# Forming expert 0's token list by itself, ahead of the gates, in a one-core encoder layer with a grouped top-2 mixture of experts

## The chip, the cores and the metric

The kernel runs on one NeuronCore of a Trainium2 chip. Five engines matter here: TensorE (PE in the profile, with its weight loads as PEld), VectorE (DVE), ScalarE (ACT), GpSimd (POOL) and SyncE (SP), which issues most DMAs. The metric is the device time of one execution in microseconds, lower is better; the number given for a kernel is the median of its runs.

## The reference, cut to what matters

A layer takes 512 tokens (two sequences of 256) of width 1024. The first part is a token mixer; its result, normalised, is `x1`. The second part, which the change touches, sends every token to 2 of 16 experts:

```python
s = sigmoid(x1 @ w_router)                       # 512 x 16
sb = (s + b_router).reshape(-1, 4, 4)            # 4 groups of 4 experts
group = argmax of the sum of the two best sb in each group
idx = the two best experts of that group
w = s[idx] / sum(s[idx])                         # the two gates of the token
for e in range(16):
    h = silu(x1 @ w_e1[e]) * (x1 @ w_e3[e])
    y += gates[:, e] * (h @ w_e2[e])             # gates are 0 where e wasn't chosen
```

The kernel doesn't compute all tokens with all experts. For each expert it forms a list of at most 128 tokens that chose it, gathers their rows, computes those, and scatters the results. (A second part for experts with more than 128 tokens stands behind a branch that this input doesn't take.)

## The kernel before

**What comes ahead.** The token mixer takes the first 440 us. TensorE then turns and multiplies the normalised rows with the router weights, and the scores of all tokens reach VectorE at 452.3 us. SyncE writes `x1` to DRAM (`x1_scratch`), since the rows of an expert are gathered from there.

**Selection, on VectorE (lines 1435 to 1478).** Small operations on 128 partitions by 16 to 64 elements make `r_sel` (1 where a token chose an expert, line 1447). From it come the gates (`w_sum`, `w_inv`, `gates`), the rank of the expert among the chosen (`r_kth`), and the table `info`, with four columns for each token and expert: the token's number plus one, which of its two choices it is, and the gate in two parts. TensorE makes `position` from `r_sel` meanwhile: the place of each token in each expert's list (lines 2103 and 2106). A token chooses from one group only, so `joint` adds the four groups' positions for the k-th expert of a group: one `onehot` matrix (token by place) then serves experts k, 4+k, 8+k and 12+k together.

**Lists.** A product of a `onehot` with `info` (`joint_slots`, line 2117: four matmuls for one k, one for each tile of 128 tokens) gives for each place of the list the token, the choice and the gate, for four experts. `fill_lists` on VectorE turns this into `list_token` (the gather's indices), `list_row` (where results go) and `list_gate`. Places without a token get a number out of bounds. In the kernel before, both first one-hots are made, then the lists of k=0 and of k=1 follow, each with its own product; those of k=2 and k=3 come later, while TensorE computes expert 0.

**Gather.** GpSimd clears `xg` (a memset of both buffers, line 1767) once `x1` is stored, and then gathers the rows of expert 0 and expert 1 (`gather`, line 1751), each as soon as its list is there (`token_ready`). TensorE turns the gathered rows (`turn_xg`, line 2137), ScalarE rounds them to `xgT_hi`, VectorE makes the rest `xgT_lo` (`split_xg`, line 1541). Every product of the expert stage needs both parts, of the rows and of the weights.

**Experts.** From there TensorE computes the experts one after the other: 12 units of weights each (512 KB a unit), which SyncE loads, ScalarE rounds to `w_hi` (line 719) and VectorE completes with `w_lo` (`cast_lo`, line 1055).

**What keeps the order.** Each engine's instructions stand in the order in which the code issues them; semaphores with constants hold them to each other. On VectorE the operations that follow the first two lists are, in this order, three `cast_lo`, the two one-hots for k=2 and k=3, and `split_xg(0, 0)`. TensorE fills waiting time with matmuls whose result nobody reads (`keep_busy`, line 2097, each 128x512).

Of the kernel before, what the change touches and what calls it, by code (L numbers as in the profile page):

```python
# [17 lines left out]
P = 128  # L18
# [143 lines left out]
def encoder_layer(nc, A, out_prompt, out_sample):  # L162
# [316 lines left out]
    def m_filled(b, n):  # L479
        return psum_full[b], n + (m_full[b] + 1)  # L480
# [564 lines left out]
    def _(dve):  # L1045
        steps = [0, 0, None]

        def step(k=1):
            steps[0] += k
            return steps[0] if steps[2] is None else steps[2] * steps[1] + steps[0]  # L1050
# [366 lines left out]
        def ranks(rank, beats, value):  # L1417

            for d in range(1, 4):
# [31 lines left out]
        sel = sel.bitcast(F32)  # L1451
        dve.wait_ge(*drained("r_s"))
        dve.tensor_tensor(r_tmp[:], r_s[:], sel, ALU.mult).then_inc(dve_step, 1)
        dve.tensor_copy(r_kth[..., 1:2], sel[..., 0:1]).then_inc(dve_step, 1)
# [3 lines left out]
        dve.wait_ge(dve_step, step(3))  # L1458
        dve.tensor_reduce(w_sum[:], r_tmp[:].rearrange("p t g e -> p t (g e)"), AX.X, ALU.add).then_inc(dve_step, 1)
        dve.tensor_tensor(r_kth[..., 2:3], r_kth[..., 1:2], sel[..., 1:2], ALU.add).then_inc(dve_step, 1)  # L1460
        dve.wait_ge(dve_step, step(2))
        dve.reciprocal(w_inv[:], w_sum[:]).then_inc(dve_step, 1)
        dve.tensor_tensor(r_kth[..., 3:4], r_kth[..., 2:3], sel[..., 2:3], ALU.add).then_inc(dve_step, 1)
        dve.wait_ge(dve_step, step(2))
        dve.tensor_tensor(gates[:], r_tmp[:].rearrange("p t g e -> p t (g e)"),
                          w_inv[:].unsqueeze(2).to_broadcast([P] + by_expert), ALU.mult).then_inc(dve_step, 1)
        dve.tensor_tensor(info[..., 1], r_kth[:].rearrange("p t g e -> p t (g e)"), chosen, ALU.mult).then_inc(
            dve_step, 1)
        dve.wait_ge(dve_step, step(2))
        dve.tensor_copy(info[..., 2], gates[:]).then_inc(dve_step, 1)  # L1470
        dve.wait_ge(*filled("position"))
        dve.scalar_tensor_tensor(out=position[:], in0=bank("position")[:, 0:64].rearrange("p (t e) -> p t e", t=TT),
                                 scalar=1.0, in1=sel.rearrange("p t g e -> p t (g e)"), op0=ALU.add,
                                 op1=ALU.mult).then_inc(routed, 1)
        dve.wait_ge(dve_step, step())
        dve.tensor_tensor(info[..., 3], gates[:], info[..., 2].bitcast(F32), ALU.subtract).then_inc(dve_step, 1)
# [3 lines left out]
        dve.wait_ge(dve_step, step(2))  # L1480

# [15 lines left out]
        def four(table, k):  # L1497
            return table[:].rearrange("p (g k) -> p k g", k=4)[:, k]

        def fill_lists(n, places):  # L1500

            dve.wait_ge(*m_filled(M_INFO, n))
            m = len(places)
            found = [psum[M_INFO][:, 16 * s:16 * s + 4 * places[s][0].shape[-1]].rearrange("p (g c) -> p g c", c=4)
                     for s in range(m)]
            none = [list_none[:, s, 0:places[s][0].shape[-1]] for s in range(m)]
            base = [list_base[:, s, 0:places[s][0].shape[-1]] for s in range(m)]
            for s in range(m):
# [3 lines left out]
            for s in range(m):  # L1512
                dve.scalar_tensor_tensor(out=places[s][0], in0=none[s], scalar=-1.0, in1=found[s][:, :, 0],
                                         op0=ALU.add, op1=ALU.add).then_inc(token_ready, 1)
                dve.scalar_tensor_tensor(out=base[s], in0=none[s], scalar=-1.0, in1=found[s][:, :, 0],
                                         op0=ALU.add, op1=ALU.add).then_inc(dve_step, 1)
# [7 lines left out]
        def joint_lists(n, *ks):  # L1524

            fill_lists(n, [(four(list_token, k), four(list_row, k), four(list_gate, k)) for k in ks])

# [21 lines left out]
        def split_hT(n, hT_hi=hT_hi[:], hT_lo=hT_lo[:]):  # L1549
# [139 lines left out]
    def _(pool):  # L1689
# [137 lines left out]
    def _(pe):  # L1827
# [327 lines left out]
        def output(n, j, k, per=0, i=None, hT_hi=hT_hi, hT_lo=hT_lo):  # L2155
# [158 lines left out]
```

## Time and profile before

| | |
|---|---|
| runs | 779.31, 778.81, 778.55 us; median 778.81 |
| the profiled execution | 777.9 us, its span 776.1 us |
| PE / PEld busy | 745.4 us (96%) / 616.5 us (79%) |
| DVE / ACT / POOL busy | 609.9 us (79%) / 432.6 us (56%) / 72.0 us (9%) |
| mean granted clock of TensorE | 0.992 |
| chain that ended last | PE 85%, DVE 8%, DMA 2%, ACT 2%, SP's queue 2%, issue 1% |

The span is the time that the profile covers, and the 1.8 us beside it lie around it. TensorE is busy in nearly all of the span. A granted clock of 1.00 is 2.4 GHz, 0.50 is 1.2 GHz.

### The profile page before, as it was taken

How to read it: one execution, taken by the hardware profiler on the slowest of the kernel's cores; microseconds unless marked ns; L12 is line 12 of the kernel's file. 1: busy time of each engine (PE TensorE's matmuls, PEld its weight loads, DVE VectorE, ACT ScalarE, POOL GpSimd, SP SyncE). 2: the span in 40 equal slices, each digit the busy share in tenths (PEclk: the TensorE clock that was granted, in tenths of full speed). 3: DMA queues.
4: the chain of work that ended last, by engine and by line, in shares of the span. 5: the costliest groups of instructions: out<-in, count | busy, mean ns of one | idle time of the engine just before them, and what ended most of it. 6: DMA issues, size and time to landing. Idle time of an engine off the chain costs nothing.

```text
span 776.1 us, 10638 instructions
## 1 busy us (share of the span) xinstructions
PE 745.4 (96%) x3516; PEld 616.5 (79%) x3516; DVE 609.9 (79%) x827; ACT 432.6 (56%) x585; POOL 72.0 (9%) x96
## 2 busy tenths in 40 slices
PE   4999999999999999999999979999999999999995
PEld 3888877887888888888888857888888888888873
DVE  5799977777678857444348888999999999999977
ACT  5522235657322335422421456888888888888851
POOL 5000000000000000000011121111111111110314
PEclk9999999999999999999999989999999999999998
DMA  9744657232343452332388587999999999999682
GB/s 297 238 98 108 204 147 205 71 93 84 109 134 109 112 167 74 115 103 88 104 303 300 186 302 255 351 392 379 388 386 389 391 400 384 381 394 378 146 171 111
DMA packets 137489, 175.51 MB, mean 226 GB/s; under 512 B 15419, under 2 KB 75559, under 8 KB 137431
## 3 DMA queue, kind: packets, MB, share of 16 engines
q1 hardware_dynamic: 128896, 154.95, 58.8%
q0 software_dynamic: 7616, 19.34, 8.3%
q10 hardware_dynamic: 934, 0.69, 0.3%
q8 instruction: 23, 0.38, 0.2%
q14 instruction: 20, 0.16, 0.1%
HBM read 164.06 MB, written 19.11 MB: 236 GB/s over the span
## 4 chain that ended last, share of the span: by engine, by line
PE 85%; DVE 8%; DMA 2%; ACT 2%; SPq 2%; issue 1%; POOL 0%; DVEq 0%; ACTq 0%; POOLq 0%
PE bank L1842 25%; PE bank L1844 25%; PE bank L1843 25%; DVE w_lo L1055 2%; PE bank L2137 2%; DMA raw<-in_w_in_dram 2%; SPq L606 1%; DVE conv L1125 1%; DVE conv_odd L1125 1%; PE bank L2058 1%; PE bank L1837 1%; PE bank L2152 1%; PE bank L2238 1%; PE bank L1888 1%; PE bank L1904 1%
## 5 line engine op out<-in xcount | busy, mean ns | idle before, releaser
L1055 DVE TENSOR_TENSOR w_lo<-raw,w_hi 128x1024 fp32r<-128x1024 f32 x103 | 125.0, 1220 | 77.2 <-ACT w_hi L719 77.1
L719 ACT CAST w_hi<-raw 128x1024 fp32r<-128x1024 f32 x103 | 107.0, 1048 | 101.5 <-PE bank L1844 97.6
L1842 PE MATMUL bank<-xT_hi,w_hi 128*128 128x512 f32 x352 | 138.5, 393 | 2.7 <-DVE xT_lo L1093 1.5
L1844 PE MATMUL bank<-xT_hi,w_lo 128*128 128x512 f32 x352 | 137.1, 390 | 0.0
L1843 PE MATMUL bank<-xT_lo,w_hi 128*128 128x512 f32 x352 | 137.0, 389 | 0.0
L1842 PE MATMUL bank<-w_hi,xgT_hi 128*128 128x512 f32 x198 | 80.1, 405 | 1.0 <-issue 1.0
L1842 PEld LDWEIGHTS bank<-xT_hi,w_hi 128*128 128x128 f32 x352 | 66.1, 188 | 17.3 <-issue 3.1
L1844 PE MATMUL bank<-w_hi,xgT_lo 128*128 128x512 f32 x198 | 77.5, 391 | 0.0
L1843 PE MATMUL bank<-w_lo,xgT_hi 128*128 128x512 f32 x198 | 77.3, 390 | 0.0
L1844 PEld LDWEIGHTS bank<-xT_hi,w_lo 128*128 128x128 f32 x352 | 66.1, 188 | 14.0
L1843 PEld LDWEIGHTS bank<-xT_lo,w_hi 128*128 128x128 f32 x352 | 66.1, 188 | 13.4
L834 ACT ACTIVATE gate<-bank,vec 128x512 f32<-128x512 f32 x24 | 16.5, 689 | 83.2 <-PE bank L1844 83.2
L1055 DVE TENSOR_TENSOR w_lo<-raw_more,w_hi 128x1024 fp32r<-128x1024 f32 x40 | 48.2, 1221 | 5.7 <-ACT w_hi L719 5.4
L1055 DVE TENSOR_TENSOR w_lo<-raw_late,w_hi 128x1024 fp32r<-128x1024 f32 x40 | 48.2, 1220 | 4.1 <-ACT w_hi L719 3.9
L1125 DVE SCALAR_TENSOR_TENSOR conv<-conv_in,conv_col,conv 128x512 f32<-128x512 f32 x60 | 44.6, 744 | 0.0
L719 ACT CAST w_hi<-raw_more 128x1024 fp32r<-128x1024 f32 x40 | 41.2, 1049 | 4.5 <-PE bank L1844 4.5
L1844 PEld LDWEIGHTS bank<-w_hi,xgT_lo 128*128 128x128 f32 x198 | 37.2, 188 | 7.9
L1842 PEld LDWEIGHTS bank<-w_hi,xgT_hi 128*128 128x128 f32 x198 | 37.3, 188 | 7.8 <-issue 1.2
L719 ACT CAST w_hi<-raw_late 128x1024 fp32r<-128x1024 f32 x40 | 41.2, 1050 | 2.5 <-PE bank L1844 2.5
L1843 PEld LDWEIGHTS bank<-w_lo,xgT_hi 128*128 128x128 f32 x198 | 37.3, 188 | 6.6
L1125 DVE SCALAR_TENSOR_TENSOR conv_odd<-conv_in,conv_col,conv_odd 128x512 f32<-128x512 f32 x56 | 41.6, 744 | 0.0
L1055 DVE TENSOR_TENSOR w_lo<-raw_rows,w_hi 128x1024 fp32r<-128x1024 f32 x32 | 38.3, 1218 | 0.0
(289 smaller groups left out, 1530.9 us busy)
## 6 DMA issues: line engine op xcount, KB each, us to landing
raw_more<-in_w_e_dram SPq DMA_DIRECT2D x48, 512.0 KB, 7.0
raw<-in_w_e_dram SPq DMA_DIRECT2D x48, 512.0 KB, 7.9
raw_late<-in_w_e_dram SPq DMA_DIRECT2D x48, 512.0 KB, 7.1
raw_rows<-in_w_e_dram SPq DMA_DIRECT2D x48, 512.0 KB, 7.9
raw<-in_w_in_dram SPq DMA_DIRECT2D x28, 512.0 KB, 6.5
raw<-in_w_gate_dram SPq DMA_DIRECT2D x24, 512.0 KB, 3.7
y_scratch<-zeros SPq DMA_DIRECT2D x8, 512.0 KB, 5.3
raw<-in_w_o_dram SPq DMA_DIRECT2D x8, 512.0 KB, 3.8
```

Of the source, the lines that this page charges most:

```text
L606: sp.dma_start(v_win[:, seq, j, :], v_grid[:, WINDOW[j]:WINDOW[j] + KCOLS, :]).then_inc(v_windows, 16)
L719: act.copy(hi_slot(j), raw_slot(j)).then_inc(hi_cast, 1)
L834: act.activation(gate[:, n if n < 2 else r % 2, d, :], bank(name)[:], ACT.Sigmoid, bias=column(V_GATE + n * DC + 2 * r + d)).then_inc(free ...
L1055: dve.tensor_tensor(lo_slot(j), raw_slot(j), hi_slot(j).bitcast(F32), ALU.subtract).then_inc(lo_cast, 1)
L1125: o = dve.scalar_tensor_tensor(out=sum_, in0=shifted, scalar=conv_col[:, k, c:c + 1], in1=sum_, op0=ALU.mult, op1=ALU.add)
L1837: o = pe.transpose(bank(name)[:, k * P:(k + 1) * P], tile(k), ident)
L1842: pe.matmul(out, hi_l, hi_r, start=start, stop=False)
L1843: pe.matmul(out, hi_l, lo_r, start=False, stop=False)
L1844: return pe.matmul(out, lo_l, hi_r, start=False, stop=stop)
L1888: o = pe.matmul(bank(("attended", g))[:, j * P:(j + 1) * P], v_win[:, seq, j, hp * P:(hp + 1) * P], probsT[:, j * P:(j + 1) * P], start=Tr ...
L1904: o = pe.transpose(bank(name)[:, tokens_of(t)], x_in[:, t, c * P:(c + 1) * P], ident)
L2137: o = pe.transpose(psum[M_XT + half][:, k * P:(k + 1) * P], xg[:, q, c * P:(c + 1) * P], ident)
```

## The change

Four things are done.

1. VectorE makes `info`'s token column, `position`, `joint` and the first one-hot ahead of the gates. A new `first_tokens` then makes only `list_token` of k=0. The gates, `r_kth` and the rest of `info` follow, and after these the second one-hot.
2. TensorE gets a new `first_slots`: four matmuls with the token column alone (4 columns for the four experts of k=0 in place of 16).
3. The full lists of k=0 and k=1 are made together from one set of eight matmuls (`joint_slots(1, 0, 1)`), and `list_token` of k=0 isn't written again there. `keep_busy(10)` is split into 5 ahead of these eight matmuls and 5 behind.
4. GpSimd clears `xg` once TensorE's mixer products are done (`unit_used` at `U_MOE`), and waits for the stored `x1` behind this.

```diff
@@ VectorE, after r_sel @@
+        dve.tensor_tensor(info[..., 0], token_one[:].unsqueeze(2).to_broadcast([P] + by_expert), chosen,
+                          ALU.mult).then_inc(dve_step, 1)
+        dve.wait_ge(*filled("position"))
+        dve.scalar_tensor_tensor(out=position[:], ...).then_inc(routed, 1)
+        dve.wait_ge(routed, 1)
+        dve.tensor_reduce(joint[:], ...)
...
+        def first_tokens():
+
+            found, none = psum[M_INFO][:, 0:4], list_none[:, 0, :]
+            dve.wait_ge(*m_filled(M_INFO, 0))
+            dve.tensor_scalar(none, found, 0.0, 65536.0, ALU.is_equal, ALU.mult).then_inc(dve_step, 1)
+            dve.wait_ge(dve_step, step())
+            dve.scalar_tensor_tensor(out=four(list_token, 0), in0=none, scalar=-1.0, in1=found, op0=ALU.add,
+                                     op1=ALU.add).then_inc(token_ready, 1)
+            dve.wait_ge(token_ready, 1)
+            dve.sem_inc(psum_free[M_INFO], 1)
+
+        make_joint(0, 0)
         dve.wait_ge(*drained("r_s"))
         dve.tensor_tensor(r_tmp[:], r_s[:], sel, ALU.mult).then_inc(dve_step, 1)
         dve.tensor_copy(r_kth[..., 1:2], sel[..., 0:1]).then_inc(dve_step, 1)
...
+        first_tokens()
+        dve.wait_ge(dve_step, step(0))
         dve.tensor_reduce(w_sum[:], ...)
...
-        make_joint(0, 0)
         make_joint(1, 1)
-        joint_lists(0, 0)
         dve.tensor_reduce(most[:], bank("position")[:, 64:80], AX.X, ALU.max).then_inc(frees("position"), 1)
-        joint_lists(1, 1)
+        joint_lists(1, 0, 1)
@@ GpSimd @@
-        pool.wait_ge(x1_stored, 16 * TT)
+        pool.wait_ge(unit_used, U_MOE)
         pool.memset(xg[:], 0.0).then_inc(pool_step, 1)
         pool.wait_ge(pool_step, 2 * TT + 2)
+        pool.wait_ge(x1_stored, 16 * TT)
         gather(0, 0, 0)
@@ TensorE @@
+        def first_slots():
+
+            pe.wait_ge(onehot_ready, 1)
+            pe.wait_ge(*m_empty(M_INFO, 0))
+            for t in range(TT):
+                rows = info[:, t].rearrange("p (g k) c -> p k g c", k=4)[:, 0, :, 0]
+                o = pe.matmul(psum[M_INFO][:, 0:4], onehot[:, 0, t, :], rows, start=t == 0, stop=t == TT - 1)
+            o.then_inc(psum_full[M_INFO], 1)
+
         pe.wait_ge(routed, 1)
-        joint_slots(0, 0)
-        joint_slots(1, 1)
-        keep_busy(10)
+        first_slots()
+        keep_busy(5)
+        joint_slots(1, 0, 1)
+        keep_busy(5)
         turn_xg(0, 0, 0)
```

TensorE, from the position products to the turn of the first gathered rows. Before (line 2117 are the list products, 2097 the unread ones, 2137 the turn):

```order
L2103 MATMUL bank<-r_sel,before_r 128x80
L2106 MATMUL bank<-r_sel,ones_r 128x64
L2106 MATMUL bank<-r_sel,ones_r 128x48
L2106 MATMUL bank<-r_sel,ones_r 128x32
L2106 MATMUL bank<-r_sel,ones_r 128x16
L2117 MATMUL bank<-info,onehot 128x16 x8
L2097 MATMUL bank<-w_hi 128x512 x10
L2137 MATMUL bank<-const,xg 128x128 x8
```

The same stretch of TensorE in the changed kernel:

```order
L2118 MATMUL bank<-r_sel,before_r 128x80
L2121 MATMUL bank<-r_sel,ones_r 128x64
L2121 MATMUL bank<-r_sel,ones_r 128x48
L2121 MATMUL bank<-r_sel,ones_r 128x32
L2121 MATMUL bank<-r_sel,ones_r 128x16
L2184 MATMUL bank<-info,onehot 128x4 x4
L2112 MATMUL bank<-w_hi 128x512 x5
L2132 MATMUL bank<-info,onehot 128x16 x8
L2112 MATMUL bank<-w_hi 128x512 x5
L2152 MATMUL bank<-const,xg 128x128 x8
```

Four matmuls of 4 columns are new, and five of the unread products now stand ahead of the eight list products, which all stand together.

VectorE, from the gates to the first list. Before:

```order
L1463 TENSOR_TENSOR r_kth<-r_kth,r_sel 128x16
L1465 TENSOR_TENSOR gates<-r_tmp,w_inv 128x64
L1467 TENSOR_TENSOR info<-r_kth,r_sel 128x64
L1470 CAST info<-gates 128x64
L1472 SCALAR_TENSOR_TENSOR position<-bank,r_sel 128x64
L1476 TENSOR_TENSOR info<-gates,info 128x64
L1478 TENSOR_REDUCE joint<-position 128x16
L1493 SCALAR_TENSOR_TENSOR onehot<-joint,iota_one 128x512 x2
L1509 TENSOR_SCALAR list_none<-bank 128x4
L1513 SCALAR_TENSOR_TENSOR list_token<-list_none,bank 128x4
```

VectorE in the changed kernel, from `r_sel` to the first list and into the gates:

```order
L1453 TENSOR_TENSOR info<-token_one,r_sel 128x64
L1457 SCALAR_TENSOR_TENSOR position<-bank,r_sel 128x64
L1460 TENSOR_REDUCE joint<-position 128x16
L1475 SCALAR_TENSOR_TENSOR onehot<-joint,iota_one 128x512
L1551 TENSOR_TENSOR r_tmp<-r_s,r_sel 128x64
L1552 COPY r_kth<-r_sel 128x16
L1542 TENSOR_SCALAR list_none<-bank 128x4
L1544 SCALAR_TENSOR_TENSOR list_token<-list_none,bank 128x4
L1556 TENSOR_REDUCE w_sum<-r_tmp 128x4
L1557 TENSOR_TENSOR r_kth<-r_kth,r_sel 128x16
```

VectorE in the changed kernel, from the last column of `info` to the first `cast_lo` and the next one-hots:

```order
L1569 TENSOR_TENSOR info<-gates,info 128x64
L1475 SCALAR_TENSOR_TENSOR onehot<-joint,iota_one 128x512
L1572 TENSOR_REDUCE most<-bank 128x1
L1491 TENSOR_SCALAR list_none<-bank 128x4 x2
L1498 SCALAR_TENSOR_TENSOR list_base<-list_none,bank 128x4
L1496 SCALAR_TENSOR_TENSOR list_token<-list_none,bank 128x4
L1498 SCALAR_TENSOR_TENSOR list_base<-list_none,bank 128x4
L1502 SCALAR_TENSOR_TENSOR list_row<-bank,list_base 128x4
L1504 TENSOR_REDUCE list_gate<-bank 128x4
L1502 SCALAR_TENSOR_TENSOR list_row<-bank,list_base 128x4
L1504 TENSOR_REDUCE list_gate<-bank 128x4
L1575 TENSOR_SCALAR overflow<-most 128x1
```

The first token list moved ahead of all of the gates; the second one-hot, which stood next to the first, moved behind them, and the operations that fill the lists in full now stand in one block. Nothing else moved on VectorE: behind this block the three `cast_lo`, two one-hots and the two parts of `split_xg(0, 0)` stand as before.

## Rows read from the trace of the kernel before

**Rows 1.** What TensorE waited for behind the start of expert 0, 468 to 776 us.

```profile
PE bank L1842 <- issue: 1.0, 1, 1.0
```

**Rows 2.** Timeline of TensorE: start us, us, engine, line, operation, tiles, count, idle before.

```profile
455.72 0.59 PE L2106 MATMUL bank<-r_sel,ones_r 128*128 128x64 f32 x4
459.49 0.99 PE L2117 MATMUL bank<-info,onehot 128*128 128x16 f32 x4 [3.17 <-issue]
461.36 0.99 PE L2117 MATMUL bank<-info,onehot 128*128 128x16 f32 x4 [0.88 <-DVE list_gate L1521]
462.21 4.36 PE L2097 MATMUL bank<-w_hi 128*128 128x512 f32 x10
466.41 1.03 PE L2137 MATMUL bank<-const,xg 128*128 128x128 f32 x8
468.46 0.47 PE L1842 MATMUL bank<-w_hi,xgT_hi 128*128 128x512 f32 x1 [1.01 <-issue]
```

**Rows 3.** Timeline of VectorE, selection to the first split of gathered rows.

```profile
455.57 0.23 DVE L1453 TENSOR_TENSOR r_tmp<-r_s,r_sel 128x64 f32<-128x64 f32 x1
455.71 1.10 DVE L1454 COPY r_kth<-r_sel 128x16 f32<-128x16 f32 x1
...
456.87 0.22 DVE L1459 TENSOR_REDUCE w_sum<-r_tmp 128x4 f32<-128x64 f32 x1
...
457.95 0.23 DVE L1470 CAST info<-gates 128x64 fp32r<-128x64 f32 x1
...
458.21 0.28 DVE L1476 TENSOR_TENSOR info<-gates,info 128x64 fp32r<-128x64 f32 x1
458.41 0.25 DVE L1478 TENSOR_REDUCE joint<-position 128x16 f32<-128x64 f32 x1
458.69 1.29 DVE L1493 SCALAR_TENSOR_TENSOR onehot<-joint,iota_one 128x512 fp32r<-128x512 f32 x2
460.52 0.16 DVE L1509 TENSOR_SCALAR list_none<-bank 128x4 f32<-128x4 f32 x1 [0.53 <-PE bank L2117]
460.71 0.16 DVE L1513 SCALAR_TENSOR_TENSOR list_token<-list_none,bank 128x4 int32<-128x4 f32 x1
...
462.39 0.16 DVE L1509 TENSOR_SCALAR list_none<-bank 128x4 f32<-128x4 f32 x1 [1.10 <-PE bank L2117]
...
463.06 2.35 DVE L1055 TENSOR_TENSOR w_lo<-raw_more,w_hi 128x1024 fp32r<-128x1024 f32 x2
...
467.67 0.69 DVE L1541 TENSOR_TENSOR xgT_lo<-bank,xgT_hi 128x512 fp32r<-128x512 f32 x1
```

**Rows 4.** Timeline of ScalarE: the rounding of the first gathered rows.

```profile
467.04 1.07 ACT L932 CAST xgT_hi<-bank 128x512 fp32r<-128x512 f32 x2 [8.21 <-PE bank L2137]
```

**Rows 5.** Timeline of GpSimd: the memset and the first gather's issue.

```profile
454.96 1.81 POOL L1767 MEMSET xg<- 128x2048 f32 x1 [11.07 <-DMA x_scratch<-x]
461.81 1.16 POOL L1751 DMA_INDIRECT xg<-x_scratch,list_token  x1 [5.03 <-DVE list_token L1513]
```

**Rows 6.** Tile xg: first two gathers (443 to 470 us), then all 16, issue to landing.

```profile
DMA to landing us min/median/max: 4.0/4.6/5.2
...
DMA to landing us min/median/max: 3.7/6.7/7.1
```

**Rows 7.** Timeline of the lists of k=2 and 3: products, VectorE's first and last row.

```profile
473.98 0.95 PE L2117 MATMUL bank<-info,onehot 128*128 128x16 f32 x8
...
475.10 0.22 DVE L1509 TENSOR_SCALAR list_none<-bank 128x4 f32<-128x4 f32 x2
...
475.97 0.16 DVE L1521 TENSOR_REDUCE list_gate<-bank 128x4 f32<-128x8 f32 x1
```

**Rows 8.** Stages: busy us of PE, PEld, DVE, ACT, POOL; granted clock, DMA share, GB/s.

```profile
459.50:466.00 6.50, 5.62 (x17) 4.78 (x18) 4.74 (x16) 0.00 (x0) 2.72 (x2) 0.50 0.84 300
...
767.20:769.50 2.30, 0.00 (x0) 0.00 (x0) 2.23 (x6) 0.00 (x0) 1.80 (x3) 1.00 0.23 91
770.00:776.00 6.00, 0.00 (x0) 0.00 (x0) 2.40 (x4) 0.00 (x0) 0.00 (x0) 0.50 0.52 200
```

More of the change, by code:

```diff
@@ L1451, in _ @@
         sel = sel.bitcast(F32)
-        dve.wait_ge(*drained("r_s"))
-        dve.tensor_tensor(r_tmp[:], r_s[:], sel, ALU.mult).then_inc(dve_step, 1)
-        dve.tensor_copy(r_kth[..., 1:2], sel[..., 0:1]).then_inc(dve_step, 1)
         chosen = sel.rearrange("p t g e -> p t (g e)")
@@ L1457, in _ @@
                           ALU.mult).then_inc(dve_step, 1)
[L1458 to L1470, printed above, removed]
+        step()
         dve.wait_ge(*filled("position"))
         dve.scalar_tensor_tensor(out=position[:], in0=bank("position")[:, 0:64].rearrange("p (t e) -> p t e", t=TT),
[L1473 to L1476, printed above, removed]
+                                 scalar=1.0, in1=chosen, op0=ALU.add, op1=ALU.mult).then_inc(routed, 1)
         dve.wait_ge(routed, 1)
@@ L1503, in fill_lists @@
             m = len(places)
-            found = [psum[M_INFO][:, 16 * s:16 * s + 4 * places[s][0].shape[-1]].rearrange("p (g c) -> p g c", c=4)
+            found = [psum[M_INFO][:, 16 * s:16 * s + 4 * places[s][1].shape[-1]].rearrange("p (g c) -> p g c", c=4)
                      for s in range(m)]
-            none = [list_none[:, s, 0:places[s][0].shape[-1]] for s in range(m)]
-            base = [list_base[:, s, 0:places[s][0].shape[-1]] for s in range(m)]
+            none = [list_none[:, s, 0:places[s][1].shape[-1]] for s in range(m)]
+            base = [list_base[:, s, 0:places[s][1].shape[-1]] for s in range(m)]
             for s in range(m):
@@ L1524, in joint_lists @@
         def joint_lists(n, *ks):
-            fill_lists(n, [(four(list_token, k), four(list_row, k), four(list_gate, k)) for k in ks])
+            fill_lists(n, [(four(list_token, k) if k else None, four(list_row, k), four(list_gate, k)) for k in ks])
         def slot_gates(q, scatters, e, n=LISTS - 1):
@@ L1553, in split_hT @@
                               ALU.subtract).then_inc(psum_free[M_HT], 1)
-        make_joint(0, 0)
+        def first_tokens():
+            found, none = psum[M_INFO][:, 0:4], list_none[:, 0, :]
+            dve.wait_ge(*m_filled(M_INFO, 0))
+            dve.tensor_scalar(none, found, 0.0, 65536.0, ALU.is_equal, ALU.mult).then_inc(dve_step, 1)
+            dve.wait_ge(dve_step, step())
+            dve.scalar_tensor_tensor(out=four(list_token, 0), in0=none, scalar=-1.0, in1=found, op0=ALU.add,
+                                     op1=ALU.add).then_inc(token_ready, 1)
+            dve.wait_ge(token_ready, 1)
+            dve.sem_inc(psum_free[M_INFO], 1)
+        make_joint(0, 0)
+        dve.wait_ge(*drained("r_s"))
+        dve.tensor_tensor(r_tmp[:], r_s[:], sel, ALU.mult).then_inc(dve_step, 1)
+        dve.tensor_copy(r_kth[..., 1:2], sel[..., 0:1]).then_inc(dve_step, 1)
+        step(2)
+        first_tokens()
+        dve.wait_ge(dve_step, step(0))
+        dve.tensor_reduce(w_sum[:], r_tmp[:].rearrange("p t g e -> p t (g e)"), AX.X, ALU.add).then_inc(dve_step, 1)
+        dve.tensor_tensor(r_kth[..., 2:3], r_kth[..., 1:2], sel[..., 1:2], ALU.add).then_inc(dve_step, 1)
+        dve.wait_ge(dve_step, step(2))
+        dve.reciprocal(w_inv[:], w_sum[:]).then_inc(dve_step, 1)
+        dve.tensor_tensor(r_kth[..., 3:4], r_kth[..., 2:3], sel[..., 2:3], ALU.add).then_inc(dve_step, 1)
+        dve.wait_ge(dve_step, step(2))
+        dve.tensor_tensor(gates[:], r_tmp[:].rearrange("p t g e -> p t (g e)"),
+                          w_inv[:].unsqueeze(2).to_broadcast([P] + by_expert), ALU.mult).then_inc(dve_step, 1)
+        dve.tensor_tensor(info[..., 1], r_kth[:].rearrange("p t g e -> p t (g e)"), chosen, ALU.mult).then_inc(
+            dve_step, 1)
+        dve.wait_ge(dve_step, step(2))
+        dve.tensor_copy(info[..., 2], gates[:]).then_inc(dve_step, 1)
+        dve.wait_ge(dve_step, step())
+        dve.tensor_tensor(info[..., 3], gates[:], info[..., 2].bitcast(F32), ALU.subtract).then_inc(dve_step, 1)
+        dve.wait_ge(dve_step, step())
         make_joint(1, 1)
-        joint_lists(0, 0)
         dve.tensor_reduce(most[:], bank("position")[:, 64:80], AX.X, ALU.max).then_inc(frees("position"), 1)
-        joint_lists(1, 1)
+        joint_lists(1, 0, 1)
         dve.wait_ge(*drained("position"))
```

6 lines of the change are left out of this document (3 added, 3 removed).

## The prediction

> **What bounds the kernel now.** I first read what TensorE waited for behind the start of the experts [rows 1]: in the 307 us from 468.46 us on there is one wait, of 1.0 us, and it is the one directly ahead of the first expert matmul. From there TensorE never stands still until its own work is done, so the end moves by whatever the start of that matmul moves by, and by nothing else on the other engines. The question is what sets 468.46.
>
> Then I read the timelines backwards from that matmul. It needs the first half of `xgT_lo`, which starts at 467.67 and takes 0.69 [rows 3]; the matmul follows 0.79 us after that start [rows 2]. `xgT_lo` in turn needs two things. One is the data: the gather is issued at 461.81 [rows 5] and lands 4.0 us later, at 465.8 [rows 6]; TensorE turns the rows from 466.41, because its ten unread matmuls (4.36 us from 462.21) are only then over [rows 2]; ScalarE starts rounding at 467.04, two casts in 1.07 [rows 4], so the first half is there at about 467.57. The other is VectorE itself. From 463.06 it runs three `cast_lo` and two one-hots, and `xgT_lo` is next in its order: from the start of the first cast to the start of `xgT_lo` it takes 467.67 - 463.06 = 4.61 us [rows 3]. The two chains end within 0.1 us of each other. The reader should see that shortening only the gather's chain gives at most this 0.1 us: a second chain of the same length stands beside it, and it starts where VectorE finishes the list of k=1.
>
> **The change, along the gather's chain.** `info`'s token column starts where `r_tmp` did, at 455.57 (0.23). The position products end at 455.72 + 0.59 = 456.31 [rows 2], which is now a wait of some 0.5 us on VectorE. `position` then takes about 0.3 to the start of `joint` (no row shows it free of neighbours; between the 0.2 of its kind and 0.35, no more than 0.1 either way). `joint` starts at 456.65, the one-hot 0.28 later (458.41 to 458.69), and one one-hot is half of 1.29: it ends at 457.58 [rows 3]. TensorE started its product 0.15 us after the end of its one-hot (459.49 against 458.69 + 0.65), so `first_slots` starts at 457.73.
>
> Four matmuls of 4 columns have no row. Four of 16 columns took 0.99 with the clock at half [rows 2, 8], and eight took 0.95 in a stretch at full clock [rows 7]. The bounds are 0 and 0.99; I take half of the eight, 0.48, since each also loads a 128-column one-hot as those did. They end at 458.21. From the start of `list_none` to the end of `list_token` before is 0.35 (460.52 to 460.87), behind a gap of 0.04 [rows 2, 3]: the list is there at 458.60. `r_tmp` and the copy to `r_kth` lie inside the wait for TensorE and cost nothing; if that cover were gone they would cost some 0.3. GpSimd issued its gather 461.81 - 460.87 = 0.94 us behind the list [rows 3, 5], so now at 459.54, which is 2.27 us earlier. It lands at 463.5 by the 4.0 of the first gather, 464.7 by the 5.2 of the second, 466.2 by the median of all 16 [rows 6]. Even at 466.2 the first half is rounded 0.63 + 0.53 us later (466.41 to 467.04, half of 1.07 [rows 2, 4]), at 467.4. The gather's chain gets 0.2 to 2.9 us of slack.
>
> **The change, along VectorE's chain.** Behind the token list come the gates. Before, from the start of `w_sum` (456.87) to the end of `info`'s last column (458.21 + 0.28) it was 1.62 us, and `position` in the middle filled a wait [rows 3]. Now they run from 458.63 to 460.25. The second one-hot ends at 460.28 + 0.65 = 460.93. The eight products start 0.15 later, at 461.08, and take 0.95 at full clock or 2 x 0.99 = 1.98 at half: they end at 462.03 or 463.06. I take full, since TensorE now has five unread matmuls (half of 4.36/2 is 1.1 us at full rate) right behind `first_slots`, so that its longest idle stretches here are 1.4 and 1.7 us, where before it had 3.17. Then the lists: ten operations took 475.10 to 476.13 = 1.03 [rows 7]; one is left out, about 0.95. The lists end at 463.02 and `cast_lo` starts at about 463.0. Before it was 463.06.
>
> The terms of this chain against before, from `r_sel` on: the stall of the copy to `r_kth` goes away. It took 1.10 us inside the memset of GpSimd, 454.96 to 456.77 [rows 3, 5], for 16 elements, where its like take 0.2: -0.9. The wait for `position` is new: +0.5. The waits for list products were 0.53 + 1.10 [rows 3] and become 0.04 + 0.15 + 0.48 less the 0.25 covered, and 0.15 + 0.95 + 0.04: -0.1. The token list of k=0 is made apart and its other parts again in the larger block: +0.4. The sum is -0.06 us, and then the fixed 4.61 puts `xgT_lo` at 467.6 and the first expert matmul at 468.4. TensorE's own additions (`first_slots`, and k=0 in the later block) all lie ahead of that wait and cost nothing by themselves.
>
> The moved memset now runs from about 443.9 (GpSimd was idle for 11.07 us before 454.96 [rows 5]) to 445.7, beside `scale_x1` on VectorE. `r_tmp`, a two-input operation of the same kind, took 0.23 in the middle of the memset [rows 3, 5], so I cost that at nothing. If such operations were held, up to 1.8 us would come into VectorE's line ahead of the scores; that row speaks against it.
>
> **The sum.** 777.9 us for the profiled execution, less 0.06, is 777.8. The profiled execution lies 0.9 below the median of the runs, 778.81. I apply the change to the median: 778.81 - 0.1 = 778.7. A measurement of this kernel can tell 0.2%, 1.6 us, from no change; this is far inside.
>
> **The rivals.**
>
> *TensorE's clock falls before the experts (slower).* The second five unread matmuls end at about 463.15, the turn ends 1.03 us behind the landing, so at 464.6 to 465.8, and then TensorE is idle until 468.4, 2.6 to 3.8 us, where before it was busy until 467.44. The trace shows two falls from 2.4 to 1.2 GHz: between the position products and 459.5, in an idle stretch of 3.17 us; and at the end, where the clock still stood at 1.00 during the idle 767.2 to 769.5 and at 0.50 from 770.0 [rows 2, 8]. So an idle stretch of some 2.3 to 3.2 us brings it, which is the stretch I get. Coming back was slow: TensorE worked almost without a break from 461.36 and was at 0.50 through 466.0, 4.6 us. If the expert matmuls start at half and stay there for 4.6 us of work, half of this is lost: 2.3 us, 781.0 (3 to 6 us: 780.2 to 781.7). Against it: the eight turn matmuls may come later, with a landing of 5.2 or more, and cut the idle time into two pieces under 2.7. It decides from an idle stretch of about 2.8 us on. Chance 0.35. The Trainium skill (TensorE: Matmul & The Clock Gate, section on why this matters for your kernels) tells authors to leave no long idle gaps between bursts of matmuls, since the clock drops to half; by that rule the time is this rival's.
>
> *The cast in `info` is held by the gather's issue (no change, a little slower).* The cast of the gates (457.95, 0.23 before [rows 3]) would start at 459.73 now, while GpSimd works on the gather from 459.54 for 1.16 us [rows 5]. The copy to `r_kth` was held until the memset ended. If the gather's issue does the same, the cast ends at about 460.9 and VectorE's chain is 0.9 longer: 779.6. For it speaks the held copy; against it, that writing descriptors is not a memset. Chance 0.08. The Trainium skill (SBUF — State Buffer, section "Who interferes with whom") says that copies and casts can take the pair of ports shared with GpSimd, whole instruction against whole instruction, and the later one waits; by it this case happens if the cast runs in that mode.
>
> *The lists come much cheaper (faster).* To pass 1.6 us, VectorE's chain from `r_sel` to `cast_lo`, 7.4 us, must shrink by that much. With both sets of products at 0 it is 1.4 us shorter, 777.3, and with the 0.9 by which unprofiled runs of before lie higher also gone, 776.4. The 2.27 us of the gather can't be won while three casts and two one-hots stand in VectorE's order ahead of the split. Chance 0.12, about 776.8.
>
> *The change does what it says, and VectorE stays the bound*, my forecast: 0.45, at 778.7, itself 778.0 to 779.4.
>
> **How the numbers follow.** The likeliest case gives 778.7. Faster is 0.12; within 0.2% are 0.45 + 0.08 = 0.53; slower 0.35. For the range I leave out most of the faster case and the top of the clock's: 777.4 to 781.4.
>
> **What would show it.** In the changed kernel: the gather's issue at about 459.5; the copy to `r_kth` at 0.2; the first of the three `cast_lo` at 463.0 within 0.3; GpSimd and ScalarE done with the first rows well before VectorE splits them, at 467.6; the first expert matmul at 468.4. The clock between 463 and 473 decides the rest: 0.50 there is the rival. The prediction is wrong if the matmul starts before 467, or if the clock is at half when it starts.

## The result and the profile after

The changed kernel takes 781.07 us (median of 7 runs, 780.55 to 783.36), the kernel before 778.67 (7 runs, 777.78 to 779.74): a ratio of 1.0034, 95% interval 1.0025 to 1.0043. It is slower by 2.4 us between the medians, 2.6 us by the ratio. Its profiled execution took 781.7 us with a span of 779.9, 3.8 more than before, at a mean granted clock of 0.986 (before 0.992).

The busy times of the whole page of the changed kernel show little; PE is 4.3 us longer with only four matmuls more:

```profile
PE 749.7 (96%) x3520; PEld 618.8 (79%) x3520; DVE 609.6 (78%) x828; ACT 432.7 (55%) x585; POOL 72.1 (9%) x96
```

The timeline of TensorE in the changed kernel (columns as in [rows 2]):

```profile
455.73 0.59 PE L2121 MATMUL bank<-r_sel,ones_r 128*128 128x64 f32 x4
457.71 0.73 PE L2184 MATMUL bank<-info,onehot 128*128 128x4 f32 x4 [1.39 <-issue]
458.30 2.48 PE L2112 MATMUL bank<-w_hi 128*128 128x512 f32 x5
461.39 1.88 PE L2132 MATMUL bank<-info,onehot 128*128 128x16 f32 x8 [0.61 <-DVE onehot L1475]
463.12 2.48 PE L2112 MATMUL bank<-w_hi 128*128 128x512 f32 x5
466.20 1.97 PE L2152 MATMUL bank<-const,xg 128*128 128x128 f32 x8 [0.60 <-DMA xg<-x_scratch,list_token]
469.65 0.76 PE L1857 MATMUL bank<-w_hi,xgT_hi 128*128 128x512 f32 x1 [1.48 <-issue]
470.21 0.63 PE L1858 MATMUL bank<-w_lo,xgT_hi 128*128 128x512 f32 x1
...
474.90 0.47 PE L1857 MATMUL bank<-w_hi,xgT_hi 128*128 128x512 f32 x1
475.21 0.40 PE L1858 MATMUL bank<-w_lo,xgT_hi 128*128 128x512 f32 x1
```

Its stages (start and end, us, then the columns of [rows 8]):

```profile
454.00:458.00 4.00, 2.01 (x13) 1.43 (x11) 3.09 (x17) 3.90 (x5) 0.00 (x0) 1.00 0.97 310
458.00:461.40 3.40, 2.79 (x9) 1.78 (x8) 2.56 (x12) 0.89 (x1) 1.16 (x1) 0.50 1.05 406
465.70:469.60 3.90, 1.97 (x8) 1.57 (x8) 3.90 (x6) 1.17 (x2) 0.67 (x1) 0.50 0.74 205
469.60:475.00 5.40, 5.35 (x13) 4.22 (x14) 1.77 (x2) 1.04 (x1) 0.00 (x0) 0.50 0.44 163
475.50:480.00 4.50, 4.50 (x25) 3.85 (x24) 3.33 (x12) 4.10 (x5) 0.00 (x0) 1.00 0.62 199
```

Read the clock column from top to bottom. It is at 1.00 until 458.0 and at 0.50 from there through 475.0 without a break. Before, it was at half only from 459.3 to 466.2, a stretch that holds the list products (0.99 us for each four [rows 2]) and no expert work. Now two kinds of needed work run at 1.2 GHz: the eight list products (1.88 us, where I had counted on the 0.95 of full rate [rows 7]), and, new against the kernel before, the first twelve expert matmuls, whose starts lie 0.43 us apart instead of 0.23.

VectorE's timeline in the changed kernel (columns as in [rows 3]):

```profile
457.66 0.17 DVE L1552 COPY r_kth<-r_sel 128x16 f32<-128x16 f32 x1
458.48 0.16 DVE L1542 TENSOR_SCALAR list_none<-bank 128x4 f32<-128x4 f32 x1 [0.65 <-PE bank L2184]
458.67 0.16 DVE L1544 SCALAR_TENSOR_TENSOR list_token<-list_none,bank 128x4 int32<-128x4 f32 x1
458.99 0.22 DVE L1556 TENSOR_REDUCE w_sum<-r_tmp 128x4 f32<-128x64 f32 x1 [0.15 <-DVE list_token L1544]
...
460.07 0.23 DVE L1567 CAST info<-gates 128x64 fp32r<-128x64 f32 x1
...
460.64 0.69 DVE L1475 SCALAR_TENSOR_TENSOR onehot<-joint,iota_one 128x512 fp32r<-128x512 f32 x1
463.31 0.23 DVE L1491 TENSOR_SCALAR list_none<-bank 128x4 f32<-128x4 f32 x2 [1.89 <-PE bank L2132]
...
464.26 2.35 DVE L1055 TENSOR_TENSOR w_lo<-raw_more,w_hi 128x1024 fp32r<-128x1024 f32 x2
...
468.86 1.28 DVE L1524 TENSOR_TENSOR xgT_lo<-bank,xgT_hi 128x512 fp32r<-128x512 f32 x2
```

The distance from the first cast to the split is 4.60 us, as before (4.61), but the cast starts at 464.26 and not at 463.06. On GpSimd the first gather is indeed issued 1.95 us earlier, and lands at 466.2, 0.4 us later than before. The issue in GpSimd's timeline, then the DMA view of the issues from 459 to 460 us with the time to landing last:

```profile
459.86 1.16 POOL L1765 DMA_INDIRECT xg<-x_scratch,list_token  x1 [14.22 <-issue]
```

```profile
xg<-x_scratch,list_token POOLq DMA_INDIRECT x1, 6.3
```

**The sum between the two profiled executions.** The position products start at the same time (455.60 and 455.59). The first expert matmul starts 1.19 us later (469.65 against 468.46). From the start of the first expert matmul to the start of the fifteenth it then takes 5.80 us (469.65 to 475.45), and in the kernel before, at full clock, 3.25 (468.46 to 471.71): 2.55 us. Together that is 3.7 of the 3.8 us by which the span grew.

### The profile page after: what moved, and what is told of

It is laid out like the page before. It is cut to its first block, busy times and chain, and to the rows that moved or that the text cites. A ratio compares the mean times of both kernels' runs of the same rounds, so it can differ in the third digit from the quotient of the medians.

```text
span 779.9 us, 10649 instructions
## 1 busy us (share of the span) xinstructions
PE 749.7 (96%) x3520; PEld 618.8 (79%) x3520; DVE 609.6 (78%) x828; ACT 432.7 (55%) x585; POOL 72.1 (9%) x96
## 4 chain that ended last, share of the span: by engine, by line
PE 78%; SPq 10%; DVE 5%; DMA 3%; ACT 2%; issue 2%; POOLq 0%; DVEq 0%; ACTq 0%
PE bank L1857 23%; PE bank L1859 23%; PE bank L1858 23%; SPq L583 6%; SPq L565 3%; DMA raw<-in_w_in_dram 2%; PE bank L2152 2%; SPq L606 1%; DVE w_lo L1055 1%; PE bank L2073 1%; SPq L590 1%; PE bank L2167 1%; PE bank L2263 1%; PE bank L1852 1%; PE bank L1903 1%
```

## Experiments

Two theories. **Clock:** the whole loss is TensorE's clock, and it comes from how the unread matmuls now lie around the list products. **Work:** the separate product and the gates behind it make the chain ahead of the experts longer. Each kernel was timed against the kernel before on the same chip (medians 778.39, 778.55 and 778.45 us in the three batches, 26 to 35 runs each). "Start" below is the time from the first position product to the first expert matmul: 12.87 before, 14.05 in the changed kernel.

| kernel | median us | ratio, 95% interval | start | clock at half around the experts' start |
|---|---|---|---|---|
| a_fill12 | 779.59 | 1.0016, 1.0007 to 1.0024 | 15.04 | 460.1 to 470.4 |
| a_fillall | 778.41 | 1.0004, 0.9995 to 1.0012 | 13.07 | none |
| a_fill_gap | 780.96 | 1.0030, 1.0020 to 1.0041 | 13.07 | 463.3 to 473.5 |
| b_fill5 | 780.73 | 1.0026, 1.0016 to 1.0035 | 13.16 | 459.5 to 473.2 |
| b_memset | 777.75 | 0.9995, 0.9983 to 1.0006 | 12.63 | 458.6 to 465.4 |
| b_fillall | 779.17 | 1.0003, 0.9993 to 1.0012 | 12.60 | 468.3 to 471.7 |
| a_fill_order | 777.99 | 0.9995, 0.9986 to 1.0004 | 12.19 | none |
| b_fill_order | 778.71 | 0.9999, 0.9989 to 1.0009 | 12.58 | none |
| b_hold | 778.39 | 0.9993, 0.9984 to 1.0002 | 12.82 | 460.0 to 466.8 |
| a_fill_order_hold | 776.14 | 0.9967, 0.9955 to 0.9979 | 11.42 | none |
| b_fill_order_hold | 776.67 | 0.9978, 0.9967 to 0.9988 | 11.50 | 460.8 to 464.2 |
| a_best | 774.70 | 0.9952, 0.9940 to 0.9965 | 10.59 | 458.1 to 461.5 |

Kernels with a_ start from the changed kernel, those with b_ from the kernel before. A ratio is estimated from all runs of both kernels and isn't the quotient of the two medians. The last two columns are each of one profiled execution, and the clock doesn't do the same in every execution of a kernel: the twelve of a_fill_gap took 778.48 to 783.40 us, with mean granted clocks of 0.992 to 0.987.

### More unread matmuls behind the lists: a_fill12

```diff
         joint_slots(1, 0, 1)
-        keep_busy(5)
+        keep_busy(12)
```

> The changed kernel with 12 unread matmuls in place of 5 behind the eight list products, nothing else. Clock theory: what the change costs is TensorE's clock, which stood at 1.2 GHz from 458.0 to 475.1 us in the trace of the changed kernel, since no long unbroken stretch of wide matmuls is left ahead of expert 0. With 12 the stretch is as long as the ten of before, the clock is back at 2.4 GHz when the expert matmuls start, and of the 3.8 us between the profiled spans the 2.5 us of half-rate expert matmuls go away: span 777 to 778, ratio to the kernel before 0.999 to 1.002. Chain theory: the longer chain on VectorE (lists ready 1.2 us later) is the cost; the ratio stays at 1.003 or more whatever the clock does.

Stages of a_fill12:

```profile
464.30:470.20 5.90, 5.90 (x16) 4.63 (x17) 5.57 (x15) 0.00 (x0) 1.70 (x1) 0.50 0.59 189
470.50:475.00 4.50, 3.49 (x18) 2.77 (x17) 1.46 (x3) 2.12 (x3) 0.00 (x0) 1.00 0.65 222
```

The clock still falls around the small products, at 460.1, but comes back at 470.4, ahead of the first expert matmul (472.03). The price moved to the start, 15.04, since twelve unread matmuls at half rate end only at 469.8 and the turn of the rows waits behind them. About half of the loss is gone. (The profiled execution is the slowest of this kernel's eleven, 782.19 us; what it shows of the start may not be typical.)

### The gaps filled: a_fillall

```diff
+        keep_busy(5)
         pe.wait_ge(routed, 1)
         first_slots()
-        keep_busy(5)
+        keep_busy(11)
         joint_slots(1, 0, 1)
-        keep_busy(5)
+        keep_busy(16)
```

> The changed kernel with unread matmuls in every gap: 5 between the position products and the first list product, 11 in place of 5 ahead of the eight products, 16 in place of 5 behind them. Clock theory: the clock stays at 2.4 GHz throughout, the eight products take 0.95 us in place of 1.88, VectorE starts its first cast at 463.0 to 463.3 in place of 464.26 and the first expert matmul is at 468.4 to 468.7: ratio 0.998 to 1.000, about 777.5 to 778.7 us. Chain theory: the first expert matmul stays at 469.5 and the ratio at 1.002 or more. A gain of over 0.2% would need the gather's chain to be the bound, which both theories deny.

Stages of a_fillall:

```profile
455.00:462.00 7.00, 6.28 (x34) 4.99 (x35) 4.48 (x20) 3.56 (x4) 1.16 (x1) 1.00 1.05 395
462.00:468.00 6.00, 4.60 (x24) 3.55 (x23) 5.93 (x16) 1.07 (x2) 1.71 (x1) 1.00 0.69 215
468.00:475.00 7.00, 6.69 (x33) 5.69 (x34) 4.40 (x6) 4.32 (x4) 0.00 (x0) 1.00 0.63 210
```

The whole change is in this kernel, and nothing but unread matmuls was added. The clock stays at 1.00, the cast starts at 462.91, which is 7.67 us behind the first position product (before 7.47), and the loss is gone: 1.0004. Within the interval, keeping the clock up gives back the whole loss against the kernel before. It also tests the prediction's sum, which had the clock at full: start 13.07 against 12.87, so +0.2 us where I had -0.06. It doesn't show that the rearranged work is free, since the kernel before has its own list products at half rate; what the work costs at equal clock is read from b_fill_order below.

### Only the first gap filled: a_fill_gap

```diff
+        keep_busy(5)
         pe.wait_ge(routed, 1)
         first_slots()
         keep_busy(5)
         joint_slots(1, 0, 1)
         keep_busy(5)
```

> The changed kernel with 5 unread matmuls added between the position products and the first list product, nothing else. In the changed kernel the clock fell at 458.0, during these products. Clock theory, if that fall comes from the idle 1.4 us ahead: the clock stays up through the list products, which take 0.95 us, and the ratio goes from 1.0034 to 1.000 to 1.002 (the idle time ahead of expert 0 can still bring a fall). If the fall comes from all the gaps together, the ratio stays above 1.002.

Timeline of TensorE, then stages, of a_fill_gap:

```profile
462.34 1.06 PE L2132 MATMUL bank<-info,onehot 128*128 128x16 f32 x8 [1.68 <-DVE onehot L1475]
463.25 2.48 PE L2112 MATMUL bank<-w_hi 128*128 128x512 f32 x5
```

```profile
456.00:463.00 7.00, 4.57 (x26) 3.39 (x25) 4.84 (x22) 3.91 (x5) 1.16 (x1) 1.00 1.04 374
469.70:473.40 3.70, 3.62 (x9) 2.88 (x10) 0.69 (x1) 0.74 (x2) 0.00 (x0) 0.50 0.69 252
```

The first list product (0.58 us) and the eight (1.06) now run at full rate, and the start is 13.07, as in a_fillall. But the clock falls at 463.25, behind the next idle piece of 1.68 us, and nearly four microseconds of expert matmuls run at half: 1.0030. So filling one gap only moves the fall; the time is the same as that of the changed kernel within the intervals.

### The kernel before with five unread matmuls less: b_fill5

```diff
         joint_slots(1, 1)
-        keep_busy(10)
+        keep_busy(5)
```

> The kernel before with 5 unread matmuls in place of 10 behind the two list products, nothing else of the change. Clock theory: the shorter stretch of wide matmuls doesn't bring the clock back before expert 0, so the first 10 to 20 expert matmuls run at half rate: 1 to 3 us slower, ratio 1.001 to 1.004, with the first expert matmul still at 468.5. Chain theory: VectorE's chain is untouched, the ratio is 1.000.

Stages of b_fill5:

```profile
463.20:469.70 6.50, 4.49 (x15) 3.11 (x15) 5.98 (x12) 1.15 (x2) 2.35 (x2) 0.50 0.78 253
469.70:473.10 3.40, 3.40 (x8) 2.76 (x9) 0.69 (x1) 0.44 (x2) 0.00 (x0) 0.50 0.73 251
```

No part of the change is here but that only five unread matmuls stand behind the lists. That alone costs 0.26%, most of the change's 0.34%. The kernel before had ten of them in one piece from 462.21, and its clock came back at 466.2; with five it came back at 473.2, behind eight expert matmuls. The start moved too, by 0.29 us (12.87 to 13.16), which I hadn't expected: the turn of the rows ran at half rate (1.97 us in b_fill5, 1.03 before).

### The memset alone: b_memset

```diff
-        pool.wait_ge(x1_stored, 16 * TT)
+        pool.wait_ge(unit_used, U_MOE)
         pool.memset(xg[:], 0.0).then_inc(pool_step, 1)
         pool.wait_ge(pool_step, 2 * TT + 2)
+        pool.wait_ge(x1_stored, 16 * TT)
```

> The kernel before with the memset of xg moved ahead of the wait for the stored x1, nothing else of the change. The copy to r_kth takes 0.2 us in place of 1.10, and the lists of k=0 and k=1 come 0.9 us earlier; the scores on VectorE are not delayed. Both theories: VectorE's chain gets 0.9 us shorter, but the gather and the ten unread matmuls are moved with it, so the first expert matmul is at 467.6 to 467.9 and the ratio 0.999. If the moved memset held VectorE beside scale_x1, the scores would come up to 1.8 us later and the ratio be 1.001 to 1.002.

The start is 0.24 us shorter and the ratio can't be told from 1. VectorE's chain gets shorter and the gather's then ends last: the split waits 0.48 us for ScalarE in b_memset's timeline.

```profile
467.24 1.29 DVE L1541 TENSOR_TENSOR xgT_lo<-bank,xgT_hi 128x512 fp32r<-128x512 f32 x2 [0.48 <-ACT xgT_hi L932]
```

### Is the order on VectorE the bound, and what is the separate list worth: a_fill_order, b_fillall, b_fill_order

a_fill_order is a_fillall with 12 unread matmuls in the last place, and the split moved ahead:

```diff
         cast_lo(U_MOE + 2)
+        split_xg(0, 0)
         cast_lo(U_MOE + 3)
         make_joint(2, 0)
         make_joint(3, 1)
-        split_xg(0, 0)
```

> The changed kernel with the gaps of TensorE filled (5 unread matmuls behind the position products, 11 ahead of the eight list products, 12 behind them), and on VectorE the split of the first gathered rows moved ahead of the third of the three casts and of the two one-hots. Theory that VectorE's fixed 4.6 us behind the lists is the bound: with 2.5 us of work moved behind the split, the first expert matmul starts when the gathered rows are rounded. The gather landed at 465.4 in the filled kernel, so the matmul comes at 467.5 to 467.7 in place of 468.3: ratio 0.998 to 0.9995. Rival, that the earlier list brings its full 2.3 us once VectorE is out of the way (landing 4 us behind the issue): matmul at 465.9, ratio 0.996 to 0.997. Rival, that VectorE was not the bound: ratio as in the filled kernel, 1.0004.

> The kernel before with TensorE's gaps filled: 12 unread matmuls behind the position products, 2 between the two list products, 14 in place of 10 behind them. The clock stays at 2.4 GHz, so the two list products take 0.5 us each in place of 0.99, VectorE's casts start 0.9 us earlier, and the gather lands at the same 465.8 if the queued weights set it. Then the first expert matmul is at 467.8 to 468.4: ratio 0.9985 to 1.000. If filling by itself cost something (power, or the fill running into the products), the ratio is above 1.001.

> The kernel before with the memset moved, TensorE's gaps filled (8, 2 and 14 unread matmuls) and the split of the first gathered rows moved ahead of the third cast and the one-hots: everything of a_fill_order but the separate first list. If the landing is pinned by the queued weights, the separate list brings nothing even here: the first expert matmul at 467.5 to 467.9 and the ratio within 0.0005 of a_fill_order. If the separate list brings its lead, a_fill_order is 1 us or more ahead of this one.

b_fillall is the kernel before with `keep_busy` of 12, 2 and 14 ahead of, between and behind the two list products; b_fill_order has 8, 2 and 14, this order of VectorE, and the memset of b_memset.

In a_fill_order the start is 12.19, 0.88 less than in a_fillall. (It has four unread matmuls less as well, but in a_fillall the split wasn't waiting for the rows.) The split now waits for ScalarE, which waited for the landing. The timelines of TensorE and VectorE in a_fill_order:

```profile
465.58 1.09 PE L2152 MATMUL bank<-const,xg 128*128 128x128 f32 x8 [0.53 <-DMA xg<-x_scratch,list_token]
...
467.68 0.47 PE L1857 MATMUL bank<-w_hi,xgT_hi 128*128 128x512 f32 x1 [1.01 <-issue]
```

```profile
466.89 1.29 DVE L1524 TENSOR_TENSOR xgT_lo<-bank,xgT_hi 128x512 fp32r<-128x512 f32 x2 [1.37 <-ACT xgT_hi L932]
```

That confirms VectorE's order as the bound of the changed kernel at full clock, and shows the next one 0.9 us below it: the landing. Counted from the first position product, the gather was issued 4.11 us later here and 5.13 in b_fill_order, which has both lists in the old way, and took 5.9 and 5.3 us to land. So the separate list brings the issue forward by 1.0 us, but the start only by 0.4 (12.19 against 12.58), and 0.9995 against 0.9999 can't be told apart.

The separate list also has a price on VectorE. These are the first casts of a_fillall and of b_fill_order, both at full clock and with the memset moved:

```profile
462.91 2.35 DVE L1055 TENSOR_TENSOR w_lo<-raw_more,w_hi 128x1024 fp32r<-128x1024 f32 x2
```

```profile
462.51 2.35 DVE L1055 TENSOR_TENSOR w_lo<-raw_more,w_hi 128x1024 fp32r<-128x1024 f32 x2
```

The first position products are at 455.24 and 456.63, so the casts start 7.67 and 5.88 us behind them: the list ahead of the gates makes VectorE's chain 1.8 us longer. In the change this is hidden by two gains. The moved memset gives 0.8 (7.47 before, 6.67 in b_memset), and the full clock through the lists 0.8 (6.67 in b_memset, 5.88 in b_fill_order). So the work theory is right that the chain gets longer, and wrong that this makes the loss of 0.34%: with the chain at 7.67 us, a_fillall has lost nothing against the kernel before.

b_fillall shows how much hangs on where the clock falls. It kept 1.00 through the lists and fell at 468.28, in the idle microsecond ahead of the first expert matmul at 468.41; the start gained 0.27 us, and the expert work until 471.7 ran at half. The ratio is 1.0003. Its split waited for ScalarE, so in this kernel the gather's chain ended last and not VectorE's row:

```profile
467.62 1.29 DVE L1541 TENSOR_TENSOR xgT_lo<-bank,xgT_hi 128x512 fp32r<-128x512 f32 x2 [0.44 <-ACT xgT_hi L932]
```

### The landing: b_hold, a_fill_order_hold, b_fill_order_hold

SyncE holds the weight loads from the 21st unit of the experts on until the first gather has landed:

```diff
+            if j == U_MOE + 20:
+                sp.wait_ge(gathered[0], 16)
```

b_hold is the kernel before with this alone; the other two are a_fill_order and b_fill_order with it (12 unread matmuls behind the lists in both).

> The kernel before with nothing changed but SyncE's hold of the weight loads from the 21st unit on until the first gather has landed. The landing gets shorter, about 3.1 us in place of 4.0. Theory that VectorE's chain and the unread matmuls bound the start in the kernel before: no change, ratio 0.9995 to 1.0005, first expert matmul still 12.9 us behind the position products. If the gather was the bound there, the ratio is 0.999 or less.

> As a_fill_order, and SyncE holds the weight loads from the 21st unit of the expert stage on until the first gather has landed. Theory that the gather's landing is set by the weight loads queued ahead of it (the landing took 4.0 us when issued at 461.8 and 6.3 when issued at 459.9, both at about 466): now it lands 3.5 to 4.5 us behind the issue, at about 463.3, and the first expert matmul starts at 465.9 to 466.5: ratio 0.996 to 0.998, if the weights held back are not missed later. Rival, that the landing time is the gather's own (descriptor work on GpSimd): still 6 us, no change against a_fill_order. If the weights are missed later, TensorE shows waits on the casts behind 480 us and the gain is lost.

> All of a_fill_order_hold but the separate first list: the kernel before with the memset moved, gaps filled (8, 2, 12), the split moved ahead of the third cast and the one-hots, and the weight loads held. The gather is issued 5.1 us behind the position products (4.1 in a_fill_order_hold) and lands 3.1 us later. With TensorE's unread matmuls ending at about 464.8 in both, the first expert matmul is within 0.3 us of a_fill_order_hold if these are the bound; if the separate list is what makes the gain, this one is 1 us (0.0013) slower.

The same DMA view as above, of a_fill_order_hold:

```profile
xg<-x_scratch,list_token POOLq DMA_INDIRECT x1, 3.1
```

From 5.9 us to 3.1: the held loads had kept the landing back. Without the hold SyncE issues the first of them before 455.6, four microseconds ahead of the gather. In b_hold the gather took 3.4 instead of 4.0, and the time did not move (0.9993, start 12.82), since VectorE's three casts and two one-hots still stood ahead of the split. With the order changed as well the start is 11.42 and 11.50, and the ratios are 0.9967 and 0.9978. Their intervals overlap, so the worth of the separate list is not resolved here either. TensorE's unread matmuls had become the last thing ahead of the turn in both (they ended at about 464.8), and not at the same clock: the twelve took 3.00 us in a_fill_order_hold, and in b_fill_order_hold, at half from 460.8 to 464.2,

```profile
460.16 4.58 PE L2100 MATMUL bank<-w_hi 128*128 128x512 f32 x12
```

So this pair isn't a comparison of the two lists alone.

### The best version: a_best

a_fill_order_hold with the split directly behind `cast_lo(U_MOE + 1)` and 3 unread matmuls instead of 12 ahead of the turn.

> As a_fill_order_hold, with 3 unread matmuls in place of 12 behind the eight list products, and on VectorE the split of the first gathered rows already behind the first of the three casts. In a_fill_order_hold the gather had landed at 462.7 but the turn began only at 464.84, behind the unread matmuls, and the split waited for it. Now the turn begins at 462.9, the rows are rounded at 464.1 and the cast ends at 464.4: first expert matmul at 465.1, 9.6 us behind the position products where it was 12.9 in the kernel before. Ratio 0.9945 to 0.996. If the clock falls again in the shorter fill, or the second and third cast come too late for the second and third unit, the ratio stays at 0.997 or more.

Timeline of TensorE, then of VectorE, in a_best:

```profile
457.89 4.34 PE L2114 MATMUL bank<-w_hi 128*128 128x512 f32 x11
462.07 0.95 PE L2134 MATMUL bank<-info,onehot 128*128 128x16 f32 x8
462.88 0.95 PE L2114 MATMUL bank<-w_hi 128*128 128x512 f32 x3
463.67 1.03 PE L2154 MATMUL bank<-const,xg 128*128 128x128 f32 x8
465.92 0.47 PE L1859 MATMUL bank<-w_hi,xgT_hi 128*128 128x512 f32 x1 [1.22 <-issue]
```

```profile
464.01 1.21 DVE L1057 TENSOR_TENSOR w_lo<-raw_more,w_hi 128x1024 fp32r<-128x1024 f32 x1
465.14 1.28 DVE L1526 TENSOR_TENSOR xgT_lo<-bank,xgT_hi 128x512 fp32r<-128x512 f32 x2
```

774.70 us, 0.48% under the kernel before, start 10.59 where I expected 9.6. The clock fell at 458.1 even so, the eleven unread matmuls took 4.34 instead of 2.78 us and held up the eight list products; it was back at 461.5. The split stood directly behind a cast that started only at 464.01, 8.68 us behind the first position product, so VectorE's chain was the bound again. What the same edits give without the separate list wasn't tried; as VectorE's first cast comes at 5.88 in b_fill_order and b_fill_order_hold, that version could be the faster one.

## Why the prediction was wrong

**The bound, right.** The end moved with the first expert matmul and with the clock behind it, and VectorE's row of casts set the start: the 4.61 us stayed (4.60), b_hold shortened the landing and gained nothing, a_fill_order moved the split and gained 0.88 us of start over a_fillall.

**The gather's chain, right in size, without its cause.** Issue forecast 459.54, measured 459.86; landing taken from 463.5 to 466.2, measured 466.2. The upper end came from the median of all gathers, and that it covers the measured landing is luck: I had no term for the weight loads issued ahead, which held the earlier gather until 466.2 all the same. The copy to `r_kth` took 0.17 where it had taken 1.10, as forecast.

**The gates held by the gather's issue, refuted.** The cast ran at 460.07 in 0.23 us, in the middle of the issue from 459.86 to 461.02.

**VectorE's chain, right but for the clock.** At full clock a_fillall gives +0.2 us where the sum had -0.06. In the changed kernel itself the first cast came 1.20 us later than before: -0.06 as forecast, 0.36 more in the first list (0.73 us for the four matmuls where I took 0.48, and 0.15 for the wait behind `list_token`), and 0.93 in the eight products, which come to 1.23.

**The step that failed** is "I take full, since TensorE now has five unread matmuls [...] right behind `first_slots`, so that its longest idle stretches here are 1.4 and 1.7 us, where before it had 3.17". The stretches were 1.39 and 0.61 us, and the clock fell all the same, at 458.0, and stayed at half until 475.1. That cost 0.93 us in the list products and 2.55 in the expert matmuls. I had taken two falls, both in long idle stretches [rows 8], as if only a long one could bring it; they said nothing of several short ones with small products between them. The same reading set the forecast of no change above the rival: I let it decide on the idle stretch ahead of the experts, and gave 0.35. The rival's price came close (781.0; measured 781.07), in part by luck: it was worked out for a fall behind the turn, and the fall came 7 to 10 us earlier, took in the list products as well, and lasted 17.1 us in place of some 4.6. The Trainium skill (TensorE: Matmul & The Clock Gate, the section on why this matters for your kernels) tells authors to leave no long idle gaps; the trace agrees that idle time matters, since filling the gaps kept the clock up in a_fillall, but not that a gap has to be long: the longest in the four microseconds ahead of this fall was 1.39 us.

**What I missed in the diff** is that `keep_busy(10)` had a second task. Those ten matmuls in one piece stood where the clock had already fallen [rows 2, 8] and brought it back ahead of the experts. Cut into 5 and 5 with small products between, they no longer did so. b_fill5 shows this for five behind the lists, without anything else of the change (1.0026), and a_fill12 from the other side: twelve there bring the clock back ahead of the experts.

**What stays open.** Which of the stretches brings the fall: a_fill_order and a_best have the same unread matmuls ahead of the eight list products, their start within 0.2 us, and one kept the clock while the other lost it at 458.1. So filled gaps alone don't rule the fall out. And what the separate list is worth: with the split in its old place the start is 0.47 us longer (a_fillall 13.07, b_fillall 12.60, though b_fillall also has the memset in its old place and ends with the gather's chain); with the split moved ahead it is 0.39 and 0.08 us shorter (12.19 and 12.58, 11.42 and 11.50, the last pair at unequal clock). The signs fit a shorter gather's chain beside a longer VectorE chain, but no pair of ratios resolves it.

## What to carry to other kernels

Matmuls whose result nobody reads are part of a kernel's timing: before splitting or moving them, find in the granted clock which stretch they keep or bring back, and price the critical matmuls behind it at half rate. An earlier issue of a gather is worth little while loads issued ahead of it hold its landing back and while other work stands in front of its consumer. Here the hold and the new order of VectorE had to go together: alone b_hold moved the start by 0.05 us, with both it was 11.50 without the earlier list and 11.42 with it. The rest, down to 10.59, came with fewer unread matmuls and the split further ahead. Moving one small result ahead also has a price for all that stands behind it on the same engine, here 1.8 us. Look for it even where the sum comes out at zero, since gains of other parts of the edit can hide it. When two chains end within 0.1 us of each other, expect each single edit to measure as no change.

## What the hardware showed unexpectedly

- The clock fell behind short idle pieces: 1.39 us in the changed kernel, 1.68 us in a_fill_gap, 1.21 and 1.01 us with the turn of the rows between them in b_fillall. In b_fill_order_hold it fell at 460.8 behind pieces of 0.46 and 0.32 us among small products, and in a_best at 458.1 with no piece over 0.80 us in the six microseconds before. In the changed kernel it came back only after 17.1 us, though two groups of five unread matmuls and the eight list products ran in that time.
- The time from a gather's issue to its landing moved from 6.3 (changed kernel) and 5.9 (a_fill_order) to 3.1 us (a_fill_order_hold) with the 512 KB loads from the 21st unit on held back until it had landed.
- Some profiled executions (a_fill12, b_fill5, b_hold, b_fill_order, a_fill_gap) have one more stretch at half clock at about 19.6 to 22.9 us, which puts the position products some 1.0 to 1.4 us later; that is why "start" above is counted from the position products, and why spans were compared only between before and after, which both lack it. Stages of before, then of a_fill_gap:

```profile
19.60:22.90 3.30, 3.13 (x14) 2.36 (x13) 3.14 (x7) 3.30 (x6) 0.00 (x0) 1.00 1.00 249
```

```profile
19.60:22.90 3.30, 3.30 (x9) 2.21 (x8) 3.13 (x7) 3.30 (x6) 0.00 (x0) 0.50 0.86 246
```
